# Products of half the token width, seven for eight, in the first layers of four gated feed-forwards of a two-part transformer kernel

## What is computed

```python
D_MODEL = 1024
SEQ = 512
D_FF_2 = 2816

def swiglu(x, w13, w2):
    gate, up = jnp.split(x @ w13, 2, axis=-1)
    return (jax.nn.silu(gate) * up) @ w2
```

## Time and profile before

| what | value |
|---|---|
| median of three executions | 3256.67 us |
| span of the profiled execution | 3256.1 us |
| TensorE busy | 3198.5 us, 98% |
| VectorE busy | 1772.9 us, 54% |
| ScalarE busy | 1250.6 us, 38% |
| GpSimd busy | 136.1 us, 4% |
| share of TensorE in the chain that ended last | 80%, of it L518 70% |

### The profile page before, as it was taken

One profiled execution on the slowest core, in us unless ns is written; L12 is line 12 of the kernel. 1 busy time (PEld: TensorE's weight loads), 2 busy tenths in 40 slices (PEclk: granted clock), 3 DMA queues, 4 the chain that ended last, 5 costly groups with the idle time before them and its releaser, 6 DMA issues.

```text
span 3256.1 us, 46645 instructions
## 1 busy us (share of the span) xinstructions
PE 3198.5 (98%) x20322; PEld 2628.9 (81%) x20322; DVE 1772.9 (54%) x2127; ACT 1250.6 (38%) x1605; POOL 136.1 (4%) x134
## 2 busy tenths in 40 slices
PE   9999999999999999999999999999999999999998
PEld 7887787888788888987888887888777777788886
DVE  6456766774454435463644357444666656654437
ACT  3357544443232223442422244223336554332224
POOL 2100000000000001000100011000120000100001
PEclk9999999999999999999999999999999999999999
DMA  5211222222232223222222222222222000232231
GB/s 194 99 53 65 104 91 91 92 103 89 92 104 91 89 96 126 91 78 97 91 99 83 98 99 88 95 95 89 84 80 101 16 4 15 84 104 91 88 106 65
DMA packets 47211, 286.68 MB, mean 88 GB/s; under 512 B 6416, under 2 KB 6688, under 8 KB 21408
## 3 DMA queue, kind: packets, MB, share of 16 engines
q1 hardware_dynamic: 44960, 279.51, 24.7%
q0 software_dynamic: 2048, 4.20, 0.4%
HBM read 277.39 MB, written 2.10 MB: 86 GB/s over the span
## 4 chain that ended last, share of the span: by engine, by line
PE 80%; DVE 5%; ACT 2%; issue 1%; POOL 0%; DVEq 0%; ACTq 0%
PE ps L518 70%; PE ps L3700 3%; PE ps L3738 1%; PE ps L1242 1%; DVE wl L336 1%; ACT wh L320 1%; PE ps L1243 1%; PE ps L1244 1%; DVE xl L3174 0%; PE ps L2790 0%; PE ps L985 0%; DVE tmp L3182 0%; DVE conv L2473 0%; PE ps L3745 0%; PE ps L3777 0%
## 5 line engine op out<-in xcount | busy, mean ns | idle before, releaser
L518 PE MATMUL ps<-xh,wh 128*128 128x512 f32 (+1 forms) x2464 | 966.1, 392 | 13.1 <-DVE xl L3174 3.4
L518 PE MATMUL ps<-xl,wh 128*128 128x512 f32 (+1 forms) x2464 | 941.9, 390 | 3.3 <-POOL xl L3071 3.0
L518 PE MATMUL ps<-xh,wl 128*128 128x512 f32 (+1 forms) x2464 | 910.3, 391 | 0.3 <-DVE wl L336 0.3
L336 DVE TENSOR_TENSOR wl<-raw,wh 128x2048 fp32r<-128x2048 f32 (+2 forms) x283 | 590.4, 2086 | 424.0 <-ACT wh L320 423.7
L320 ACT CAST wh<-raw 128x2048 fp32r<-128x2048 f32 (+1 forms) x280 | 485.9, 1735 | 283.7 <-PE ps L518 275.4
L518 PEld LDWEIGHTS ps<-xh,wh 128*128 128x128 f32 (+1 forms) x2464 | 462.4, 188 | 122.3 <-issue 18.7
L518 PEld LDWEIGHTS ps<-xl,wh 128*128 128x128 f32 (+1 forms) x2464 | 461.7, 188 | 105.1 <-POOL xl L3071 3.8
L518 PEld LDWEIGHTS ps<-xh,wl 128*128 128x128 f32 (+1 forms) x2464 | 461.8, 188 | 99.4 <-issue 1.0
L518 PE MATMUL ps<-hid_h,wh 128*128 128x512 f32 x880 | 342.9, 390 | 1.2 <-DVE wl L336 1.2
L518 PE MATMUL ps<-hid_l,wh 128*128 128x512 f32 x880 | 342.4, 389 | 0.0
L518 PE MATMUL ps<-hid_h,wl 128*128 128x512 f32 x880 | 342.4, 389 | 0.0
(11 more groups left out here) (494 smaller groups left out, 4017.7 us busy)
## 6 DMA issues: line engine op xcount, KB each, us to landing
raw<-in_up SPq DMA_DIRECT2D x88, 1024.0 KB, 4.7
raw<-in_down SPq DMA_DIRECT2D x64, 704.0 KB, 4.1
raw<-in_up_c SPq DMA_DIRECT2D x22, 1024.0 KB, 4.7
raw<-in_down_c SPq DMA_DIRECT2D x16, 704.0 KB, 4.0
raw<-in_gates SPq DMA_DIRECT2D x8, 1024.0 KB, 4.7
raw<-in_gv SPq DMA_DIRECT2D x8, 1024.0 KB, 4.8
raw<-in_gu SPq DMA_DIRECT2D x8, 1024.0 KB, 4.7
raw<-in_gout SPq DMA_DIRECT2D x8, 1024.0 KB, 4.7
```

Source lines behind the costliest of these rows:

```text
L336: nc.vector.tensor_tensor(wl[:, slot, 0:w], raw[:, slot, 0:w], wh[:, slot, 0:w].bitcast(F32), ALU.subtract).then_inc(lo_ready, 1)
L518: last = nc.tensor.matmul(out, stationary, moving, start=(fresh and q == 0), stop=(t == kt - 1 and half == per - 1 and q == 2), skip_group ...
```

## The change

The chunk is laid out in four quarters of 128x512: for the pairs j = 0 to 3 of input tiles, gate or value columns (the two rows of a 2x2 block matrix) by even or odd tile of the pair (its columns). The tokens are cut into a first and a second half of 256. Gate and value of both halves are then a product of two 2x2 block matrices, which takes eight block products. From unit PLAIN = 3 on, units make seven (Winograd's form of Strassen's method): 7 products, for 4 pairs, in three parts, are 84 matmuls of 128x256 for 48 of 128x512. Units 0 to 2 stay as they were, with another order of columns; so does the convolution's feed-forward (`quarters=True`).

What the form needs beside the products:

- for each feed-forward once, four sums of quarter states (`terms`, 16 tiles of 128x256 from `h` and the gain): 4 on ScalarE, the rest on VectorE (`terms_of`), then their high parts (`term_high`, ScalarE) and low parts (`term_low`, two on GpSimd, two on VectorE);
- for each unit, four sums of weight quarters on GpSimd (`sums_of`), and the splits of three plain quarters and of the four sums (`plain_high`, `sum_high` on ScalarE, `plain_low`, `sum_low` on VectorE) in place of `split_hi` and `split_lo`;
- for each unit, a copy of the first product on ScalarE (`copy_first`), seven additions or subtractions of 128x256 from PSUM on VectorE (`evict`) and one multiplication by the factor, 128x1024 (`scale`).

The product of opened gate and value (`hide`) goes to GpSimd for units 3 to 19 and stays on VectorE for the other five. The hidden tiles are kept whole and split in pairs near the end (`hidden_high` on ScalarE, `hidden_low` on VectorE, and on GpSimd for pairs 1, 4 and 7) for the second layer. The embedding's small input is split in unit 2 of the second layer, where it was in unit 5 of the first.

```diff
@@ class SwigluUp, in the place of swiglu() @@
+        def scalar(self):
+            @block.scalar
+            def _(act):
+                norm, a = self.norm, self.a
+                norm.act(act)
+                for j in range(KPAIRS):
+                    nc.scalar.activation(terms[:, j, T1, :], h[:, 2 * j, LATER], ACT.Copy,
+                                         scale=vec[:, norm.gain + 2 * j:norm.gain + 2 * j + 1]).then_inc(t_start.sem, 1)
+                norm.squares_act(act)
+                self.term_high(act, 0)
+                self.term_high(act, 1)
+                n = a + 2
+                split_hi(act, n, 16 * (n // 2 + 1), n % 2, order[n][2])
+                self.term_high(act, 2)
+                self.term_high(act, 3)
+                self.plain_high(act, 3)
+                norm.scale_act(act)
+                self.sum_high(act, 3, 0)
+                self.open(act, 0)
+                self.sum_high(act, 3, 1)
+                self.open(act, 1)
+                for unit in range(2, KF - 2):
+                    self.plain_high(act, unit + 2)
+                    self.sum_high(act, unit + 2, 0)
+                    self.open(act, unit)
+                    self.sum_high(act, unit + 2, 1)
+                    self.copy_first(act, unit + 1)
...
+        def sums_of(self, pool, unit):
+            n, k, x = self.a + unit, unit - PLAIN, self.slot(unit)
+            pool.wait_ge(raw_ready[n % 2], 16 * (n // 2 + 1))
+            pool.wait_ge(chunks_used, n + 1 if unit > PLAIN else self.a + 3)
...
+            nc.gpsimd.tensor_tensor(s1, a21, a22, ALU.add).then_inc(w_sum.sem, 1)
+            nc.gpsimd.tensor_tensor(s3, a11, a21, ALU.subtract).then_inc(w_sum.sem, 1)
+            pool.wait_ge(chunks_used, n + 1)
+            pool.wait_ge(w_sum.sem, w_sum.after(k, 1))
+            nc.gpsimd.tensor_tensor(s2, s1, a11, ALU.subtract).then_inc(w_sum.sem, 1)
+            pool.wait_ge(w_sum.sem, w_sum.after(k, 3))
+            nc.gpsimd.tensor_tensor(s4, a12, s2, ALU.subtract).then_inc(w_sum.sem, 1)
...
+        def gpsimd(self):
+            @block.gpsimd
+            def _(pool):
+                self.norm.pool(pool)
+                for j in range(2):
+                    self.term_low(pool, nc.gpsimd, pool_low, j)
+                for unit in range(PLAIN, KF):
+                    self.sums_of(pool, unit)
+                    if unit >= PLAIN + 2:
+                        self.hide(pool, nc.gpsimd, unit - 2)
+                for p in self.POOL_PAIRS:
+                    self.hidden_low(pool, nc.gpsimd, pool_low, p)
...
+        def evict(self, dve, unit):
+            k, b = unit - PLAIN, self.first_bank(unit)
+            r = [ps[:, b + i // 2, i % 2 * (T // 2):(i % 2 + 1) * (T // 2)] for i in range(7)]
...
+            dve.wait_ge(u_copied.sem, u_copied.after(k, 1))
+            dve.wait_ge(chunks_used, self.a + unit + 3)
+            nc.vector.tensor_tensor(v1, g1, r[5], ALU.add).then_inc(u_added.sem, 1)
...
+        def vector(self):
+            @block.vector
+            def _(dve):
+                norm, a = self.norm, self.a
+                norm.dve(dve)
+                split_lo(dve, a + 1, (a + 1) % 2, order[a + 1][2])
+                self.terms_of(dve, 0)
+                norm.squares_dve(dve)
+                self.terms_of(dve, 2)
+                norm.scale_dve(dve)
+                split_lo(dve, a + 2, a % 2, order[a + 2][2])
...
+                for unit in range(PLAIN, KF - 2):
+                    self.evict(dve, unit)
+                    self.scale(dve, unit)
+                    self.plain_low(dve, unit + 2)
+                    self.sum_low(dve, unit + 2, 0)
+                    self.sum_low(dve, unit + 2, 1)
+                self.evict(dve, KF - 2)
+                self.scale(dve, KF - 2)
+                n = a + KF
+                split_lo(dve, n, n % 2, order[n][2])
+                for p in (0, 2, 3, 5):
+                    self.hidden_low(dve, nc.vector, s_low, p)
+
+        def dve(self, dve):
+            n = self.a + KF + 1
+            self.hidden_low(dve, nc.vector, s_low, 6)
+            split_lo(dve, n, n % 2, order[n][2])
+            self.evict(dve, KF - 1)
+            self.scale(dve, KF - 1)
+            self.hidden_low(dve, nc.vector, s_low, 8)
+            self.hide(dve, nc.vector, KF - 2)
+            self.hidden_low(dve, nc.vector, s_low, 9)
+            self.hide(dve, nc.vector, KF - 1)
+            self.hidden_low(dve, nc.vector, s_low, 10)
...
+        def quad_waits(self, pe, unit, i):
+            if i == 0:
+                pe.wait_ge(psum_read.sem, self.read + (1 if unit == PLAIN else unit - 1))
+                pe.wait_ge(w_low.sem, w_low.after(unit - PLAIN, 1))
...
+            if i == 3:
+                pe.wait_ge(w_low.sem, w_low.after(unit - PLAIN, 2))
...
+            if i == 5:
+                pe.wait_ge(lo_ready, self.a + unit + 1)
```

More of the change, by code:

```diff
@@ L28 @@
 HALF = KF // 2
+KPAIRS = KD // 2
+QUARTERS = (1, 2, 0, 3)
 SLOT = 2048
@@ L58, in pair_chunks, with pair_column @@
 def pair_chunks(w):
-    return w.reshape(KD, P, 2, KF, P).transpose(3, 1, 0, 2, 4).reshape(KF, P, KD * 2 * P)
+    w = w.reshape(KPAIRS, 2, P, 2, KF, P).transpose(4, 2, 3, 1, 0, 5).reshape(KF, P, 4, KPAIRS * P)
+    return w[:, :, [QUARTERS.index(n) for n in range(4)]].reshape(KF, P, KD * 2 * P)
+def pair_column(t, m):
+    return QUARTERS[2 * m + t % 2] * KPAIRS * P + t // 2 * P
 def half_chunks(w):
@@ new lines, in _build @@
+    SOON, LATER = slice(0, T // 2), slice(T // 2, T)
+    PLAIN = 3
+    T3, T1, T2, T4 = range(4)
+    S3, S1, S2, S4 = range(4)
+    t_start, t_made, pool_low, w_sum, w_high, w_low, u_first, u_copied, u_added, u_scaled, u_opened, u_hidden = (
+        sb_zc, sb_abs, sb_exp, sb_ln, sb_keep, sb_cut, sb_self, sb_open, sb_after, sb_arg, sb_a, sb_out)
+    hid = area("hid", [P, KF - 2, T], 0)
+    hid_r = area("hid_r", [P, KF - 2, T], 0, F32R)
+    terms_h = area("terms_h", [P, KPAIRS, 4, T // 2], 40 * KB, F32R)
@@ new lines, in _build, with __init__ @@
+    terms = area("terms", [P, KPAIRS, 4, T // 2], 56 * KB)
+    terms_l = area("terms_l", [P, KPAIRS, 4, T // 2], 56 * KB, F32R)
+    last_hid, last_hid_r = place("last_hid", [P, 2, T], offset=x_at + 28 * KB), place("last_hid_r", [P, 2, T], F32R, offset=x_at + 28 * KB)
+    class Slot:
+        def __init__(self, at_, last_at):
+            w = KPAIRS * P
+            self.sums_h = place("sums_h", [P, 4, w], F32R, offset=at_)
+            self.plain_h = place("plain_h", [P, 3, w], F32R, offset=at_ + 8 * KB)
+            self.plain_l = place("plain_l", [P, 3, w], F32R, offset=at_ + 14 * KB)
+            parts = (at_ + 20 * KB, last_at)
+            self.sums = [place("sums", [P, 2, w], offset=o) for o in parts]
+            self.sums_l = [place("sums_l", [P, 2, w], F32R, offset=o) for o in parts]
@@ L2502, in gain, with feed_forward @@
         return VEC["norm"] + (layer * 8 + n) * KD
-    def feed_forward(layer, n, norm, between={}, sums=None):
-        linear(f"up_{layer}{n}", KD, 256, x_split, norms=norm, between=between, paired="filled", **swiglu(norm))
-        linear(f"down_{layer}{n}", HALF, P, hid_split, halves=True, norms=Made(lambda t: 4 * t + 4),
-               **(sums or summing(ybuf, 1)))
+    def feed_forward(layer, n, norm, embeds=False, sums=None):
+        up = SwigluUp(f"up_{layer}{n}", norm)
+        linear(f"down_{layer}{n}", HALF, P, up.split, halves=True, second_ahead=True, norms=up,
+               between=embedding(layer) if embeds else {}, **(sums or summing(ybuf, 1)))
     def post(source, layer, n, total=None):
@@ L2857, in _build @@
     gmlp(pre(0, 2, post(ybuf, 0, 1)))
-    feed_forward(0, 1, pre(0, 4, post(ybuf, 0, 3)), embedding(0))
+    feed_forward(0, 1, pre(0, 4, post(ybuf, 0, 3)), embeds=True)
     embed(0, Beside(gain(0, 6), post(ybuf, 0, 5)))
@@ L4170, in _build @@
     rwkv()
-    feed_forward(1, 1, pre(1, 4, post(r_out, 1, 3)), embedding(1))
+    feed_forward(1, 1, pre(1, 4, post(r_out, 1, 3)), embeds=True)
     embed(1, Beside(gain(1, 6), post(ybuf, 1, 5)))
```

324 lines of the change are left out of this document (299 added, 25 removed).

## The result

The changed kernel takes **3352.3 us** (median of 4 runs, 3351.1 to 3356.1) against 3256.3 for the kernel before (4 runs): a ratio of 1.030, interval 1.028 to 1.031. The forecast was 3321 us with a range of 3228 to 3342. The direction was right; the time lies 31 us above the forecast and 10 us above the range.

The account below looks back on a forecast made before the run. The prediction took TensorE's matmuls, busy 98% of the span, to bound the kernel. Per feed-forward, −15.2 (products) + 9.7 (turns) + 14.6 (start) + 7 (end) = +16.1 us, four times +64, gave 3321 us, range 3228 to 3342.

Parts of the forecast that it names:

- Products: Units 3 to 21: 84 matmul steps of 0.120 us, 10.08 us for 10.88; −15.2 us per feed-forward.
- Rival D: 256-wide products paced by weight loads at 0.192 us, 16.1 us a unit, total over 3650 us; chance 0.02.
- The turns: VectorE with SBUF operands and GpSimd alternate, each waiting out the other's instruction; 1.16 us per GpSimd operation.
- rival A: Cheap turns of 0.90 us: steady units need 9.34 us, TensorE stays the bound; 3251 us, chance 0.20.
- Rival B: Turns hardly matter; only the order at the start costs, 6.6 us; 3222 us, chance 0.20.
- The period: Steady units: five GpSimd turns plus VectorE's 4.84 us make 10.64 us against TensorE's 10.08; +9.7 us per feed-forward.
- When TensorE is paced: First-layer units: TensorE runs ahead to product 5, waits for the last low part, paced at 10.64 us from about unit 12.
- The start: First three units: extra sums and turns delay the terms to 1580.5 and the norm's factor; +14.6 us, bounds 6.6 and 14.6.
- rival C: Clock falls after TensorE's 10 us standstill in unit 2; +5 us per feed-forward, 3341 us; chance 0.05.
- The end: Hidden pairs end about 20.9 us after TensorE's last product, delaying the second layer; +7 us, bounds 0 and 8.

Follow-up runs that it names:

- e2: Changed kernel, but from unit 5 on GpSimd makes only 16 of 512 columns of each weight sum (output of other weights): 3287.3 us.
- e3: Changed kernel, but from unit 5 on the third and fourth weight sums, right behind the evictions, and the product go to VectorE: 3288.0 us.
- e7: e3 with five plain units, factor ahead of terms, no GpSimd work before unit 5, hidden low parts on VectorE and the end reordered: 3213.4 us.
- e10: e9 with another order on VectorE and ScalarE, GpSimd's two sums still beside the evictions; control for e11: 3207.2 us.
- e1: Changed kernel with the product of opened gate and value of units 3 to 19 back on VectorE: 3316.0 us.
- e5: e3 with the first two weight sums on VectorE too, so GpSimd has nothing from unit 5 on: 3342.3 us.
- e4: Changed kernel, but at a stage's start GpSimd waits for VectorE's last token term before its two low parts and unit 3's sums: 3339.7 us.
- e9: e7 plus one hidden low part on GpSimd beside unit 21's evictions, and the second layer's third weight piece split earlier: 3203.9 us.
- e11: e10 with one more wait: from unit 7 GpSimd's two sums start after VectorE's scaling, beside its operations with SBUF operands: 3343.3 us.

## Why the prediction was wrong in size and right in kind

*Products: right.* Steps of 0.120 us, 84 a unit: 10.08 us wherever nothing else is in the way (e2, e3, e7 to e10). Rival D is out.

*The turns: right.* GpSimd's hold on VectorE is 1.1 us in the steady units (e1), where I took 1.16 and put the deciding point of rival A at 1.05. Rival A's 0.90 is out. Rival B fell at the start already, where the terms end 36.0 us after the first matmul; I had 36.4.

*The period: the step that failed.* "Together 5 × 1.16 + 4.84 = 10.64 us of turns in a unit of 10.08." That sum asks how long the shared way to SBUF is taken, and lets VectorE's evictions run free beside it. But VectorE is one queue, and the evictions are part of it: its period is its own 7.7 us and each turn that falls on it. Of the five GpSimd operations two stand beside evictions and cost nothing; three turns of 1.10 make 11.0. The same sum gives 10.5 in e1 (8.3 + 2 × 1.10), and e5, with no turn, has its own work alone, 10.85. By it, rival A's turns of 0.90 would have paced the units too: the deciding point is (10.08 − 7.7) / 3 = 0.79 us a turn, not 1.05. The 0.36 us a unit come to 6 us in 17 units; 4.4 of them show in the stage, −1.1 for −5.5.

*When TensorE is paced: wrong, and without a price.* I had it run ahead to product 5 and be paced from about unit 12. Its units start every 10.08 us up to unit 7 and every 11.0 from unit 8 on, while VectorE's evictions are over 10.08 us apart from unit 3 on. It waits 0.69 us for the plain low parts at the head of a unit, 56 times in the four layers, since those are needed 7.2 us earlier than the last low parts. As VectorE's end sets the stage's end, where TensorE waits costs nothing.

*The start: near, with two errors against each other.* +13.2 in the first feed-forward, +16.5 to +17.3 in the others, for 14.6: 1.3 us more on average. In up_01 the interleaving went as walked. What is over is the clock. From the start of the factor's matmul to that of the 22nd matmul of the unit behind it, the kernel before takes 5.66 us, the changed kernel 7.82 in up_01 and up_10 and 8.6 in up_00 and up_11; in up_01 the granted clock is 0.50 from 1604 to 1609. So rival C happened, at 2.2 to 3.0 us and not 5, since the clock is back after about 3 us. In e4, where the wait before the factor is 1.1 to 3.1 us instead of 8.3 to 10.1, the same stretch takes 5.75 us in three feed-forwards and 7.5 in up_01, where the clock was low already. A first fall in up_01, to 0.50 between 1590 and 1594, costs nothing, because TensorE waits for the factor anyway. Without the clock the start costs 14.3 to 14.4 us in three feed-forwards and 10.2 in up_00. There, before the change, VectorE idles 5.3 us ahead of the mean (L868) and in up_01 1.2; these 4.1 us more of slack take up the delay by the first eight sums (4.4 us in my walk), which I had priced from up_01 for all four. So part of the small error is luck: the clock, left out of the sum, and up_00's slack, not looked at, stand against each other. My 1580.5 is also not the sum beside it: 1572.1 + 9.3 is 1581.4, and the terms' turns took about 8.3. In e9 the granted clock is 1.00 over the whole start, from 1530 to 1590.

*The end: right, 1.9 us too small.* +8.9 for +7. The last low part ends 20.6 us behind the last product, where I had 20.9; I had not counted the wait for the third piece of weights (1.68 us), which stands behind it and which e9 takes away.

Of the 31 us between forecast and result 4 × 4.4 are the period's, 4 × 1.3 the start's and 4 × 1.9 the end's.

The Trainium skill, "SBUF — State Buffer", section "Who interferes with whom", also says that a VectorE instruction with at most one SBUF input does not contend with GpSimd, as long as it isn't in one of the modes that use two ports. The runs agree: in e3 the evictions keep 0.41 us and GpSimd its 1.30 side by side, and e11 against e10 puts 2.05 us a unit on the difference. I had that rule before me, as the seven evictions that "take no turns", and used it only to leave them out of the sum. It is the way to make the change pay: that is where GpSimd's work belongs.
